# Router and expert tokens from unnormalised values, attention scores of two heads side by side, and the convolution on GpSimd, in a two-block transformer kernel

## What is computed

```
ux = (rms_norm(x, norm1) * (1 + sc1) + sh1) @ w_in          # split into f, q, k, v, b, c, h
attn = na_latent(q * scale, k, v, kc, vc, rpb)              # 8 heads of 64, one softmax over 512 keys
conv = b * short_conv(c * h, w_conv)                        # width 3 over positions, 256 channels
x = x + g1 * (concat([fourier_mix(f) @ w_fourier, attn, conv]) @ w_out)
hx2 = rms_norm(x, norm2) * (1 + sc2) + sh2
g_logits = hx2 @ w_rg + b_rg ; e_logits = hx2 @ w_re + b_re # 4 groups of 8 experts: best group, best 2 in it
for e in range(32):
    y += combine[:, e] * ((silu(hx2 @ w_gate[e]) * (hx2 @ w_up[e])) @ w_down[e])
x = rms_norm(x + g2 * y, norm_final)
```

## Time and profile before

| | |
|---|---|
| median of 3 runs (range) | 1753.14 us (1749.47 to 1753.19) |
| the profiled execution: its time, and the span of its trace | 1755.4 us, 1753.6 us |
| mean granted clock of TensorE | 0.916 |
| busy: PE, DVE, ACT, POOL | 1389.8, 783.5, 453.4, 314.5 us |
| moved by DMA | 582.87 MB, mean 332 GB/s |

### The profile page before, as it was taken

The page is one execution under the profiler, slowest core; times in us unless marked ns, Lnnn a source line. Parts: engine busy times, 40 slices in busy tenths (PEclk is TensorE's granted clock), DMA queues, the critical chain, the costliest instruction groups (busy, mean ns, idle before and its releaser), DMA issues.

```text
span 1753.6 us, 18769 instructions
## 1 busy us (share of the span) xinstructions
PE 1389.8 (79%) x6944; PEld 794.6 (45%) x6944; DVE 783.5 (45%) x1883; ACT 453.4 (26%) x1195; POOL 314.5 (18%) x260
## 2 busy tenths in 40 slices
PE   6999998996878787779988776889976656665666
PEld 3467885586434443335554322566732212221222
DVE  2103754326777787798788875325310000000003
ACT  1111123302434343355444343124111000100010
POOL 0000000001534454434545454000000000000000
PEclk8999999998999998999999999889878888888887
DMA  9556228735999999999999999441259999999995
GB/s 398 226 219 255 103 97 324 300 120 223 422 423 421 422 421 422 420 390 366 417 421 419 418 422 416 182 159 44 96 237 428 428 429 427 429 429 427 430 429 237
DMA packets 60120, 582.87 MB, mean 332 GB/s; under 512 B 6672, under 2 KB 7056, under 8 KB 7952
## 3 DMA queue, kind: packets, MB, share of 16 engines
q1 hardware_dynamic: 21600, 306.66, 42.5%
q0 software_dynamic: 36864, 268.45, 37.2%
q10 hardware_dynamic: 1584, 6.83, 1.0%
HBM read 580.87 MB, written 1.05 MB: 332 GB/s over the span
## 4 chain that ended last, share of the span: by engine, by line
PE 45%; DMA 37%; DVE 10%; ACT 4%; issue 3%; POOL 1%; SPq 0%; DVEq 0%; ACTq 0%
PE ps L906 40%; DMA big<-peer_uv,big 18%; DMA big<-w_stream 10%; DMA slab<-w_stream 8%; DVE big L1934 3%; PE ps L1152 2%; PE ps L1160 1%; POOL big L559 1%; ACT big L780 1%; DVE big L1945 1%; ACT big L776 1%; PE ps L1063 0%; DVE big L1882 0%; DVE stat L1798 0%; DVE big L1885 0%
## 5 line engine op out<-in xcount | busy, mean ns | idle before, releaser
L906 PE MATMUL ps<-big 128*128 128x512 f32 (+3 forms) x1914 | 601.9, 584 | 218.4 <-ACT big L780 138.3
L906 PEld LDWEIGHTS ps<-big 128*128 128x128 f32 (+1 forms) x1914 | 252.3, 180 | 539.9 <-ACT big L780 232.8
L559 POOL DMA_INDIRECT big<-peer_uv,big x256 | 314.3, 1228 | 773.8 <-DVE big L1918 424.4
L1934 DVE CUSTOM_DVE_ANT_0 big<-big 128x1024 f32<-128x1024 f32 x256 | 310.9, 1226 | 122.7 <-DMA big<-peer_uv,big 119.0
L906 PE MATMUL ps<-slab,big 128*32 128x512 f32 x1024 | 151.9, 736 | 71.3 <-DMA slab<-w_stream 47.1
L906 PE MATMUL ps<-hT,slab 128*128 128x128 f32 (+1 forms) x1216 | 182.1, 308 | 0.0
L906 PEld LDWEIGHTS ps<-hT,slab 128*128 128x128 f32 x1216 | 168.5, 191 | 19.4 <-issue 10.0
L772 ACT ACTIVATE big<-big 128x1 f32<-128x1 f32 x256 | 51.5, 201 | 346.5 <-DVE big L1934 346.0
L906 PEld LDWEIGHTS ps<-slab,big 128*32 128x32 f32 x1024 | 33.2, 124 | 177.0 <-issue 86.4
L2110 DVE TENSOR_TENSOR big<-big,ps 128x512 f32<-128x512 f32 x8 | 5.5, 687 | 229.3 <-PE ps L906 229.3
L906 PE MATMUL ps<-slab,hT 128*128 128x256 f32 (+2 forms) x304 | 91.4, 457 | 7.7 <-issue 4.7
(11 more groups left out here) (300 smaller groups left out, 1211.0 us busy)
## 6 DMA issues: line engine op xcount, KB each, us to landing
slab<-w_stream SPq DMA_DIRECT2D x113, 2048.0 KB, 18.2
big<-w_stream SPq DMA_DIRECT2D x32, 2048.0 KB, 23.1
big<-peer_uv,big POOLq DMA_INDIRECT x256, 11.9
big<-rpb ACTq DMA_DIRECT2D x1, 1536.0 KB, 11.3
cst<-consts ACTq DMA_DIRECT2D x1, 1312.0 KB, 17.5
xT<-x_t SPq DMA_DIRECT2D x1, 1024.0 KB, 5.7
hcT<-ctx_t SPq DMA_DIRECT2D x1, 1024.0 KB, 26.1
scratch<-sub_keys ACTq DMA_DIRECT2D x1, 1024.0 KB, 11.2
```

What stands on the lines that cost most here:

```text
L559: nc.gpsimd.indirect_dma_start(out=uv[b], out_offset=None, in_=peer_uv, in_offset=bass.IndirectOffsetOnAxis(ap=idxu[:, s:s + 1], axis=0)). ...
L906: ins = nc.tensor.matmul(*a, **kw)
L1934: V.tensor_tensor_reduce(out=u, in0=u, in1=xtok, scale=1.0, scalar=0.0, op0=ALU.mult, op1=ALU.add, accum_out=dots[:, s:s + 1]).then_inc(do ...
```

## The change

It has four parts.

- **Scores in pairs.** Both attentions issue scores(u + 2) and scores(u + 3) together at every even u, once both banks have been read. The first unit of the second block gets buffers of its own (`first_logit`, `first_probs`), since `hT` is still read.
- **Order at the start of attention(1).** The second half of the last projection moves behind the first two scores (`last_projection`), and ACT empties its bank behind the first exponential.
- **Convolution on GpSimd.** DVE's eight operations become twelve in `block.gpsimd`, behind all row gathers; SP's load into `extra[1]` waits for them and for the first transposed unit, since it overwrites their buffers.
- **Router and tokens from unnormalised values.** The gain is multiplied into the router weights ahead of time, and the shift's part of the logits is summed into `shift_row`. The router matmuls read `xT` itself and stand between the banks of the output projection. The sum of squares comes per token (1 column) instead of broadcast over 256, most of it added up on DVE; the logits are scaled by it in one step. The token-major copy is of `xT`, scaled by ACT per token; gain and shift are applied to the gathered `xg` in the loop, in four pieces on DVE and four on ACT. The gather of turn t + 1 stands at the end of turn t, and the first one ahead of the loop, before the rounds are computed. ACT does a one-element Silu (`warm`) at the top of each turn.

The diff, cut to its core:

```diff
@@ gpsimd, behind the row gathers
+            pool.wait_ge(bank_emptied, UNITS_B1 + UNITS_B2)
+            wc = colv("w_conv")
+            step(G.tensor_tensor(ucv, gbc[:, 512:1024], hcv, ALU.mult))
+            halves = [(ucv[:, j * T:(j + 1) * T], vcv[:, j * T:(j + 1) * T], scr[:, j * T:(j + 1) * T]) for j in range(2)]
+            for j, (u, v, w) in enumerate(halves):
+                G.tensor_scalar(v, u, wc[:, 3 * j + 1:3 * j + 2], None, ALU.mult)
+                step(G.tensor_scalar(w, u, wc[:, 3 * j:3 * j + 1], None, ALU.mult))
...
+            G.tensor_tensor(catT[:, 1536:2048], gbc[:, 0:512], vcv, ALU.mult).then_inc(conv_ready, 1)
@@ scalar, the loop
-                    act.wait_ge(gathered, t + 2)
+                    nc.scalar.activation(warm, rms2[:, 0:1], ACT.Silu)
+                    act.wait_ge(gathered, t + 1)
+                    for k in range(4, KD):
+                        ins = nc.scalar.activation(xg[:, k * P:(k + 1) * P], bank(3, P, (k - 4) * P), ACT.Identity,
+                                                   bias=modc(1, 3, k), scale=gain[:, k:k + 1])
+                    ins.then_inc(xg_high, 1)
@@ tensor, attention
-                    if u + 2 < first + UNITS:
+                    if u % 2 == 0 and u + 2 < first + UNITS:
+                        pe.wait_ge(scaled, u + 2)
                         scores(u + 2)
+                        scores(u + 3)
@@ tensor, from the output projection on
+            for b in range(4):
+                w = weights(S_OUT2 + b // 2).rearrange("p (k n) -> p k n", k=KD)
+                for j in range(2):
+                    chain(bank(b, T, j * T), by_feature(catT, w, 2 * (b % 2) + j), y_filled if j else None)
+                if b % 2:
+                    slab_done()
+                if b:
+                    router(b - 1)
+                if b == 2:
+                    turn_tokens(0)
+            router(3)
+            turn_tokens(1)
...
+            gather(1)
             pe.wait_ge(rounds_ready, 1)
@@ tensor, the end of a turn of the loop
                         mm(bank(4 + c // 2, T, (c % 2) * T), ye[:, c * P:(c + 1) * P], selT, start=False, stop=True,
                            skip_group_check=True, signal=bank_summed if c % 2 else None)
+                    gather(t + 2)
             norm(8)
@@ vector
-            dve.wait_ge(bank_emptied, UNITS_B1 + UNITS_B2)
...
-            V.tensor_tensor(catT[:, 1536:2048], gbc[:, 0:512], vcv, ALU.mult).then_inc(conv_ready, 1)
+            step(V.tensor_tensor(shifted.rearrange("p (k n) -> p k n", k=KD), w3, per_feature(modp(1, 3)), ALU.mult))
+            V.tensor_reduce(shift_sum, shifted.rearrange("p (k n) -> p n k", k=KD), X, ALU.add).then_inc(shift_summed, 1)
+            step(V.tensor_tensor(w3, w3, per_feature(gain[:, :]), ALU.mult))
             attention(1, aN2)
-            residual(4, 1, 2, 7, ybase=2 * KD)
-            norm(7, xT, hT, colv("g2"), modp(1, 4))
+            for t in range(NT):
+                ins = V.scalar_tensor_tensor(out=lg[:, t, :], in0=bank(4 + t, nr), scalar=rms2[:, t:t + 1], in1=shift_row,
+                                             op0=ALU.mult, op1=ALU.add)
```

More of the change, by code:

```diff
@@ L860, in _ @@
                 turned(8 + n, catT[:, (1 + n) * 512:(2 + n) * 512])
-            norm(7, hT, lambda k: modc(1, 3, k, 0))
-            for n in range(2):
-                turned(10 + n, xN[:, n * 512:(n + 1) * 512])
+            act.wait_ge(norm_inv, 8)
+            nc.scalar.activation(rms2, rms2, ACT.Sqrt).then_inc(norm_rstd, 1)
+            act.wait_ge(norm_rstd, 8)
+            for n in range(4):
+                t, half = n % 2, n // 2
+                act.wait_ge(turn_filled, 11 + n)
+                nc.scalar.activation(xN[:, t * D + half * 512:t * D + (half + 1) * 512], bank(turn_bank(10 + n)), ACT.Copy,
+                                     scale=rms2[:, t:t + 1]).then_inc(turn_stored, 1)
             act.wait_ge(rexp_in, 1)
@@ L1378, in _ @@
             pe.wait_ge(four_stored, 3)
+            pe.wait_ge(shift_summed, 1)
+            mm(bank(0, nr), ones, shift_sum, start=True, stop=True, signal=shift_filled)
             for j in range(2):
@@ L1391, in _ @@
             pe.wait_ge(conv_ready, 1)
[L1392 to L1395, removed]
-                for t in range(NT):
-                    mm(bank(t, nr), hT[:, k * T + t * P:k * T + (t + 1) * P], wr[:, k * nr:(k + 1) * nr], start=k == 0,
-                       stop=k == KD - 1, signal=router_filled if k == KD - 1 and t == NT - 1 else None)
-            def turn_tokens(n):
-                turn(10 + n, [hT[:, (4 * (n % 2) + k) * T + (n // 2) * P:(4 * (n % 2) + k) * T + (n // 2 + 1) * P]
-                              for k in range(4)])
@@ L1417, in _, with gather @@
             chain(bank(1, NE, 2 * NE), [(ones, sel32[:, 0:NE]), (ones, sel32[:, NE:2 * NE])], counts_filled)
-            pe.sem_inc(gathered, 1)
+            for b in range(2, 4):
+                mm(bank(4 + b), ones, zeros512, start=True, stop=True)
             pe.sem_inc(bank_summed, 4)
+            def gather(t):
+                pe.wait_ge(sel_ready, t)
+                for b in range(NT):
+                    nc.tensor.transpose(bank(2, P, b * P), selw[:, b * P:(b + 1) * P], ident)
+                for k in range(KD):
+                    chain(bank((0, 3)[k // 4], P, (k % 4) * P),
+                          [(xN[:, b * D + k * P:b * D + (k + 1) * P], sel[:, b * P:(b + 1) * P]) for b in range(NT)],
+                          gathered if k == KD - 1 else gathered_low if k == 3 else None)
+            gather(1)
             pe.wait_ge(rounds_ready, 1)
-            pe.wait_ge(turn_stored, 14)
             def expert_weights(j, i):
@@ L2119, in _ @@
             norm(8, xT, yfin, colv("g_final"), None)
-NORM_SCALED = [KD * i for i in range(8)] + [8 * KD]
-NORM_DONE = [KD * i for i in range(9)]
+NORM_SCALED = [KD * i for i in range(7)]
+NORM_DONE = [KD * i for i in range(8)] + [7 * KD]
 def constants():
```

181 lines of the change are left out of this document (118 added, 63 removed).

## The result

The changed kernel takes 1709.67 us (median of 4 runs, 1707.06 to 1711.51) against 1753.16 for the kernel before on the same chip: ratio 0.9755, interval 0.9737 to 0.9773. That is 43.5 us less where 38.3 were forecast. The mean granted clock is 0.916 in both profiled executions, but not in the same places.

The account below looks back on a forecast made before the run. DMA bounds the expert loop and row stage, so only stretches where DMA isn't full count. 10.0 + 5.5 + 12.0 + 7.4 + 6.4 - 3.0 = 38.3 us; 1755.4 becomes 1717.1, as median 1715; range 1706 to 1729.

Parts of the forecast that it names:

- Step 1: Attention(0): seven more score pairs overlap, 6.8 us, and fewer PE waits for DVE, 3.2 us; together 10.0 us gained.
- Step 2: Start of attention(1): scores ahead of the last projection cover DVE's logits, first transpose at 1170.1; 5.5 us gained.
- Step 3: Units of attention(1): score pairs give 5.0 us, PE's clock no longer falling after idle 7.0; together 12.0 us gained.
- Step 4: Convolution on GpSimd: between 4.3 and 15 us, done before the output projection reads it, so cost 0.
- Step 7: Tail: a ninth gather on PE delays the last norm sums, which then run together; 3.0 us lost.
- Step 6: Router logits to first expert matmul: earlier selection 7.2, gather 4.5, PE start 1.8, so 13.5 against 19.9; 6.4 us gained.
- Step 5: Last projection matmul to router logits: router matmuls between banks, shorter norm work; 7.5 against 14.9, 7.4 us gained.
- a rival: Slower than before: clock at half speed through attention(1) and the projection, adding up to 64 us, 1779; chance 0.03.
- the rival of engines in each other's way: Attention(1) units: GpSimd's convolution and DVE block each other, DVE stands up to 15 us, total 1730; chance 0.05.

Follow-up runs that it names:

- the order-only run: The kernel before with only the loop's scores issued in pairs in both attentions: 1728.26 us, ratio 0.9877 to the kernel before.
- the filled kernel: The kernel before with two unread matmuls added ahead of each PE wait for DVE's sums in attention(0): 1754.9 us, ratio 1.0016.

## Why the prediction was right, and where its numbers were off

The forecast of 1715 was 5.3 us high, within its range of 1706 to 1729. The lower end of the range stood for a warm gather and no clock dips in attention(0), and both came. The mechanism held in steps 1 to 4 and 7, and in step 6 but for its last term; in step 5 one of its two causes is worth nothing. The misses partly cancel, which is luck: steps 1 and 6 gave 7.3 us more than forecast, steps 2, 3 and 5 gave 1.7 less.

- **Step 1** (10.0 forecast, 15.2 measured) left out a term. Overlap was 7.8 instead of 6.8: a single score costs 1.12 by its own record where I took the chain's 1.05. I had subtracted a pair's record from two steps of the chain; measured alike, seven pairs save 7.3 us by steps from start to start (1.05 for one score, 1.06 for a pair) and 7.8 by records. Waits were 3.5 instead of 3.2, with three left instead of four. Not counted were 3.3 us of clock. The row that showed it stood in the earlier trace rows, 0.96 over 78 us; I used it for the range and as ground for a rival, and put no price on it. That the waits cause it is shown by the filled kernel; how much they cost varies, with 1.7 us less in the version without pairs, so part of the 15.2 is the luck of the profile of before. The three terms are 14.6 of the 15.2; the rest is not assigned.
- **Step 2** (5.5, measured 5.4) held; the wait that I put at about 1 us is 1.06.
- **Step 3** (12.0 = 7.0 clock + 5.0 pairs, measured 11.4 = 6.6 + 4.9) held in both terms. It rested on one thing that the order-only run shows not to be fixed: with the same idle the clock came back within four microseconds. The 6.6 us are what that stretch cost in the profile of before, not what 5.67 us of idle must cost.
- **Step 4** (0) held. The convolution took 11.6 us on GpSimd, 1154.37 to 1165.94, between the bounds of 4.3 and 15, and was done 24 us ahead of its reader. DVE's operations beside it kept their durations, 0.42 and 0.41 us for the logits' two, so the rival of engines in each other's way did not happen. None of DVE's large operations in that stretch reads two operands from SBUF, so what such a one would meet is not shown. In the new order the convolution on DVE costs 7.6 us (9.8 by the ratios), so the cover was worth having.
- **Step 5** (7.4, measured 6.4) is the one too high: the end took 5.7 us from 1220.9 to the logits' copy at 1226.58 instead of 4.8, at half clock behind the 0.83 us wait. The matmuls standing between the banks, one of the two causes that I gave, are worth nothing: behind the projection they do as well or better. What gains is that the logits no longer wait for norm, scaling and shift; that is argued from the rows of before, since the old router was not put into the changed kernel.
- **Step 6** (6.4, measured 8.5): 7.2 us to the selection came out to the tenth; the gather took 3.9 instead of 4.5, and the last term, 1.8 us until PE starts, was 0. The table load, half of its 2.61, ran while PE gathered, with and without the warming. DVE's low half was ready at 1237.57, 0.3 us before the gather ended, and reading the number of rounds cost PE nothing that the trace shows.
- **Step 7** (3.0 lost) was exact, and 3.06 come back without the ninth gather.

By the medians the parts add up: the order of scores alone saves 1.23%, all but the pairs 1.18%, together 2.41 of the 2.45 measured, each within about 0.26. By the stages they overlap: the units gain 10.0 us in the one profile and 6.6 in the other, together 5 more than the 11.4 of the change, since each took back the same half clock.

On GpSimd a product of two inputs at 128x512 took 1.27 us against DVE's 0.69, and a one-input product at 128x256 took 0.93 against 0.35; six of these are half of the 11.6 us, which is 2.7 times the 4.3 of DVE's eight operations. The GPSIMD Engine Reference of the Trainium skill (3.1, elementwise) puts two-input work at about twice DVE's time: by that rule, the trace agrees for the product of two inputs (1.27 to 0.69, 1.8 times), and the estimate of 9 us in the prediction was low by the one-input ones.

## What to carry to other kernels

Price a short wait of TensorE at more than its length where the granted clock of the stretch is below 1: the same matmuls in a stretch at clock 1.00 tell how much more it was in that execution, which need not repeat (3.3 us and 1.6 here for the same seven waits). Two half-height matmuls side by side give back nearly a whole one, but in part as waits for the next engine, so look at what its stretch allows first. When a stage at the end gets faster, follow the microseconds to the last instruction, in more than one profile: of four profiles with a small gain in the router or the tail, three gave about 2 us back in the sums behind the loop, at half clock, and two of the four were of one and the same kernel. That the gain brought the low clock is not shown.

## What the hardware showed that I had not expected

After the same idle of 5.67 us PE ran at half clock for about 14 us in the kernel before and in its version with filled waits, and for 3 to 4 in the one that differs in the order of its scores. After an idle of 4.38 us, with the convolution on DVE, it was about 4. In the same last sums of the loop the clock was full in ten profiles (3.72 us) and lower in four (5.43 to 6.14), the kernel before with its filled waits among the four, with code ahead of them that hardly differs; the kernel without the ninth gather is in both groups. What decides it stays open. GpSimd's multiplication by a per-partition scalar at 128x256 (0.93 us) is slower than its addition of two tensors at 128x255 (0.73).
